# Attention scores as three 64-row products per head, two heads alternating on the halves of the array

## What is computed

```python
scale = d ** -0.5                      # d = 64
for blk in range(S // Q):              # blocks of 128 queries
    q0, q1 = blk * Q, (blk + 1) * Q
    logits = (jnp.einsum('bhtd,bhsd->bhts', q[:, :, q0:q1], k[:, :, :q1]) * scale
              + F[:, :, q0:q1, None] - F[:, :, None, :q1])
    probs = jax.nn.softmax(jnp.where(mask, logits, -jnp.inf), axis=-1)
    outs.append(jnp.einsum('bhts,bhsd->bhtd', probs, v[:, :, :q1]))
```

## Time and profile before

| | us |
|---|---|
| median of three runs | 3614.58 |
| lowest, highest | 3612.81, 3622.89 |
| span of the profiled execution | 3614.6 |
| TensorE busy in it | 3300.8 (91%) |
| VectorE, ScalarE, GpSimd busy | 1918.7, 1224.6, 881.6 |

### The profile page before, as it was taken

One profiled execution on the slowest core, in us unless ns is written; L12 is line 12 of the kernel. 1 busy time (PEld: TensorE's weight loads), 2 busy tenths in 40 slices (PEclk: granted clock), 3 DMA queues, 4 the chain that ended last, 5 costly groups with the idle time before them and its releaser, 6 DMA issues.

```text
span 3614.6 us, 53582 instructions
## 1 busy us (share of the span) xinstructions
PE 3300.8 (91%) x19064; PEld 2868.2 (79%) x19064; DVE 1918.7 (53%) x3829; ACT 1224.6 (34%) x2043; POOL 881.6 (24%) x324
## 2 busy tenths in 40 slices
PE   8999999888888888999799989999799999999997
PEld 6878888777777777877588878887688888888875
DVE  4676566566666666014655545544564444444444
ACT  3343344333333333012344434430243333344302
POOL 2454344422222222334211010013111111111120
PEclk9899999999999999999799999999699999999997
DMA  2011011222222224411200010042021111010321
GB/s 99 35 46 46 35 41 41 102 86 75 76 81 81 81 79 176 156 65 47 93 33 33 27 39 28 27 172 78 14 79 45 45 39 39 29 39 33 115 93 58
DMA packets 63267, 235.80 MB, mean 65 GB/s; under 512 B 7216, under 2 KB 8240, under 8 KB 62144
## 3 DMA queue, kind: packets, MB, share of 16 engines
q10 hardware_dynamic: 32352, 118.58, 8.7%
q1 hardware_dynamic: 30816, 115.91, 8.7%
HBM read 184.06 MB, written 50.40 MB: 65 GB/s over the span
## 4 chain that ended last, share of the span: by engine, by line
PE 62%; DVE 17%; issue 11%; DVEq 5%; ACT 4%; DMA 1%; ACTq 1%; SPq 0%
PE ps L163 33%; PE ps L725 10%; PE ps L702 6%; DVE fox_l L978 4%; PE ps L120 3%; PE ps L686 2%; PE ps L359 2%; PE ps L687 2%; DVEq L524 2%; DVE fx_k2b L992 1%; DVE lev L503 1%; DVE nf_tri L1002 1%; PE ps L709 1%; DVE lev L514 1%; PE ps L372 1%
## 5 line engine op out<-in xcount | busy, mean ns | idle before, releaser
L184 POOL TENSOR_TENSOR w_hi<-raw,small 128x1024 fp32r<-128x1024 f32 x160 | 459.8, 2874 | 2632.1 <-PE ps L163 2526.0
L186 POOL TENSOR_TENSOR w_lo<-raw,w_hi 128x1024 fp32r<-128x1024 f32 x160 | 422.1, 2638 | 22.8
L163 PE MATMUL ps<-u_hi,w_hi 128*128 128x512 f32 x1040 | 415.0, 399 | 12.4 <-DVE u_lo L243 7.8
L163 PE MATMUL ps<-u_lo,w_hi 128*128 128x512 f32 x1040 | 410.5, 395 | 0.0
L163 PE MATMUL ps<-u_hi,w_lo 128*128 128x512 f32 x1040 | 410.5, 395 | 0.0
L163 PE MATMUL ps<-nb_u_hi,w_hi 128*128 128x512 f32 (+1 forms) x640 | 241.0, 377 | 10.2 <-DVE nb_u_lo L1389 9.9
L163 PEld LDWEIGHTS ps<-u_hi,w_hi 128*128 128x128 f32 x1040 | 197.4, 190 | 61.7 <-issue 10.6
L163 PE MATMUL ps<-nb_u_hi,w_lo 128*128 128x512 f32 (+1 forms) x640 | 237.9, 372 | 0.0
L163 PE MATMUL ps<-nb_u_lo,w_hi 128*128 128x512 f32 (+1 forms) x640 | 237.6, 371 | 0.0
L163 PEld LDWEIGHTS ps<-u_hi,w_lo 128*128 128x128 f32 x1040 | 197.5, 190 | 44.3
L163 PEld LDWEIGHTS ps<-u_lo,w_hi 128*128 128x128 f32 x1040 | 197.7, 190 | 41.9
(11 more groups left out here) (326 smaller groups left out, 7355.5 us busy)
## 6 DMA issues: line engine op xcount, KB each, us to landing
raw<-in_w_stream SPq DMA_DIRECT2D x160, 512.0 KB, 3.5
ada_w<-in_w_ada ACTq DMA_DIRECT2D x48, 512.0 KB, 6.1
nf_b<-nf_rows ACTq DMA_DIRECT2D x16, 512.0 KB, 5.7
nb_bias<-in_rel_bias ACTq DMA_DIRECT2D x16, 448.0 KB, 3.5
y_parts<-wa_y_hi ACTq DMA_DIRECT2D x8, 640.0 KB, 3.0
y_parts<-wa_y_lo ACTq DMA_DIRECT2D x8, 640.0 KB, 4.1
la_out_yh<-y_parts SPq DMA_DIRECT2D x8, 640.0 KB, 10.0
la_out_yl<-y_parts SPq DMA_DIRECT2D x8, 640.0 KB, 11.2
```

Of the source, the lines that this page charges most:

```text
L163: mm = pe.matmul(out, w(slot, tiles[i]), u[:, first + i, cols], start=start and i == 0 and p == 0, stop=stop and i == len(tiles) - 1 and p ...
L184: pool.tensor_tensor(w_hi[:, s, :], raw[:, s, :], zero, ALU.add)
L186: pool.tensor_tensor(w_lo[:, s, :], raw[:, s, :], w_hi[:, s, :].bitcast(F32), ALU.subtract).then_inc(w_ready, 1)
```

## The change

The query parts become `q_hi` and `q_lo`, the key parts `k_hi` and `k_lo`, each with the pair's first head in rows 0 to 63 and the second in rows 64 to 127, as the projection leaves them. One operation of 128 rows makes each of them, where two or four of 64 rows stood. In wa the queries change so; its keys stay as they were (both halves hold the shared head). Scores are three products of 64 rows per head, hi x hi, lo x hi, hi x lo; the fourth partial sum is no longer made. The two heads alternate, product by product, on rows 0 to 63 and 64 to 127 of the array, each into its own PSUM banks. So a pair's scores are one group on TensorE, and `plan` puts both S steps of the next pair ahead of the transposes of an odd head step: S0 S1 T.. S2 S3 T.. T.. S4 S5. The group waits until all earlier shifts are done. In wa both heads' scores now wait for `a_g`, in nb for `b_vc`, for which only the second head's did.

```diff
-                self.steps = [("S", u) for u in range(min(ahead, self.NA))]
+                self.steps = [("S", u) for u in range(2)]
...
                 for u in range(self.NA):
-                    if u + ahead < self.NA:
-                        self.steps.append(("S", u + ahead))
+                    if u % 2 and u + 2 < self.NA:
+                        self.steps += [("S", u + 1), ("S", u + 2)]
...
-                    if step[0] == "S":
+                    if step[0] == "S" and step[1] % 2 == 0:
                         u = step[1]
                         blk = self.blocks[u // 2]
-                        pe.wait_ge(self.shifted, it * self.NA + max(u - 1, 0))
+                        pe.wait_ge(self.shifted, it * self.NA + u)
...
-                        q = self.q2[u % 2][:, blk["b"] * P:(blk["b"] + 1) * P]
-                        for pc, kc, n in blk["runs"]:
-                            o = ps[:, (u % 2) * 2 * CH + pc:(u % 2) * 2 * CH + pc + n]
-                            pe.matmul(o, q, k2a[u % 2][:, kc:kc + n], start=True, stop=False)
-                            mm = pe.matmul(o, q, k2b[u % 2][:, kc:kc + n], start=False, stop=True)
-                        mm.then_inc(self.scored, 1)
+                        qc = slice(blk["b"] * P, (blk["b"] + 1) * P)
+                        for i, (pc, kc, n) in enumerate(blk["runs"]):
+                            products = ((self.q_hi, k_hi), (self.q_lo, k_hi), (self.q_hi, k_lo))
+                            for p, (q, k) in enumerate(products):
+                                for hd in range(2):
+                                    r = rows_of(hd)
+                                    mm = pe.matmul(ps[:, hd * 2 * CH + pc:hd * 2 * CH + pc + n], q[r, qc],
+                                                   k[r, kc:kc + n], start=p == 0, stop=p == 2)
+                                    if p == 2 and i == len(blk["runs"]) - 1:
+                                        mm.then_inc(self.scored, 1)
...
-                for hd in range(2):
-                    for half in range(2):
-                        ins = dve.tensor_tensor(fx_k2b[hd][rows_of(half), :], bank(2, 2)[rows_of(hd)],
-                                                fx_k2a[hd][0:HD, :].bitcast(F32), ALU.subtract)
-                ins.then_inc(f_lo, 1)
+                dve.tensor_tensor(fx_k_lo[:], bank(2, 2), fx_k_hi[:].bitcast(F32), ALU.subtract).then_inc(f_lo, 1)
...
-                    wa.pe(pe, it, [wa_k2a[g // 2]] * 2, [wa_k2b[g // 2]] * 2, [(wa_v, rows_of(g // 2))] * 2,
-                          {("S", 0): [(a_lo, j * 5 + (g + 2))],
-                           ("S", 1): [(a_g, it + 1)]})
+                    wa.pe(pe, it, wa_k2a[g // 2], wa_k2b[g // 2], [(wa_v, rows_of(g // 2))] * 2,
+                          {("S", 0): [(a_lo, j * 5 + (g + 2)), (a_g, it + 1)]})
...
-                      {("S", 1): [(b_vc, it + 1)],
+                      {("S", 0): [(b_vc, it + 1)],
```

More of the change, by code:

```diff
@@ L920, in fox_pe @@
                 mm.then_inc(f_vt, 1)
-                fox.pe(pe, it, fx_k2a, fx_k2b, [(fx_v, rows_of(hd)) for hd in range(2)],
+                fox.pe(pe, it, fx_k_hi, fx_k_lo, [(fx_v, rows_of(hd)) for hd in range(2)],
                        {("S", 0): [(f_lo, it * 2 + 2)],
@@ L943, in fox_act @@
                 act.wait_ge(w_used, it * 4 + (U_FOX + 1))
[L944 to L946 removed]
+                nc.scalar.activation(fox.q_hi[:], bank(0, 2), ACT.Copy, scale=HD ** -0.5).then_inc(f_hi, 1)
                 act.wait_ge(fox.chunk, it * 4 + 2)
                 act.wait_ge(w_used, it * 4 + (U_FOX + 2))
[L949 to L952 removed]
+                nc.scalar.copy(fx_k_hi[:], bank(2, 2)).then_inc(f_hi, 1)
                 load_ada(1)
@@ L1492, in wa_act @@
                     act.wait_ge(a_turned, j * 5 + (g + 2))
-                    for hd in range(2):
-                        ins = nc.scalar.copy(wa.q2[hd][rows_of(hd), :], wa.y[rows_of(hd), :])
-                    ins.then_inc(a_hi, 1)
+                    nc.scalar.copy(wa.q_hi[:], wa.y[:]).then_inc(a_hi, 1)
                     act.wait_ge(wa.chunk, j * 20 + 2 * (4 + 2 * g))
@@ L1568, in build_program @@
         ph7 = ctx.enter_context(ExitStack())
[L1570 to L1571 removed]
+        nb_k_hi = sb("nb_k_hi", [P, TC], F32R, ph7)
+        nb_k_lo = sb("nb_k_lo", [P, TC], F32R, ph7)
         nb_v = sb("nb_v", [P, 10, P], at=ph7)
@@ L1603, in nb_pe @@
                 mm.then_inc(b_vt, 1)
-                nb.pe(pe, it, nb_k2a, nb_k2b, [(nb_v, rows_of(hd)) for hd in range(2)],
-                      {("S", 1): [(b_vc, it + 1)],
+                nb.pe(pe, it, nb_k_hi, nb_k_lo, [(nb_v, rows_of(hd)) for hd in range(2)],
+                      {("S", 0): [(b_vc, it + 1)],
                        ("V", 0): [(b_g, it + 1)]})
```

51 lines of the change are left out of this document (13 added, 38 removed).

## The result

The kernel after takes 4008.6 us (median of 4, 3995.6 to 4025.9) where the kernel before takes 3613.7 us (3603.1 to 3622.9). The ratio is 1.109, with an interval of 1.105 to 1.113: slower by 395 us. The forecast was 3855 us, in a range up to 3960. It had the direction and missed the size by 154 us. The profiled execution has a span of 4001.5 us, 387 more than before.

The account below looks back on a forecast made before the run. TensorE, busy 91% of the span, was taken as the bound. The terms -61+11+54+208-4+30 = +238 us on 3614.6 us gave 3853, stated as 3855 us (chance 0.48), with a range of 3765 to 3960 us.

Parts of the forecast that it names:

- The products, -61: Score products on TensorE: the two halves overlap fully, 182 us in place of 243, so -61 us.
- the second half's load, +11: Weight load of the second half at the head of each score group, half of 0.108 us x 208 pairs: +11 us.
- Between full and half array, +54: TensorE going over to 64 rows and back, 0.30 us x 208 pairs, 8 less in nb: +54 us.
- The order, +208: TensorE waits longer at transposes as ScalarE does both heads' exp before copying: +208 us, bounds +150 and +250.
- Fewer copies in fox, -4: VectorE's dropped subtractions at a fox iteration's head: 0.5 of 4.9 us gained, eight times, -4 us.
- The sum without the clock: The terms -61+11+54+208-4 for the attentions; fox, wa and nb iterations some 6, 10 and 9 us longer.
- The clock, +30: Lower TensorE clock after waits at the head of nearly every wa and nb iteration: 16x1.9 = +30 us, bounds 0 and +80.
- Loads in turn: Rival: every weight load of the score products takes its turn, +90 us on the sum, 3945 us; chance 0.24.
- no overlap: Rival: score products on the two halves do not overlap at all, +171 us on the sum, 4025 us; chance 0.10.
- Smaller waits: Rival: TensorE's waits come to half of the 208 us, with no clock loss, 3720 us; chance 0.12.
- Not slower: Rival: copies arrive in time, crossings and waits together under 0.29 us per pair, down to 3550 us; chance 0.06.
- The signs: Expected profile: nb 320-column pair scores 1.2 to 1.4 us, copy waits 50 to 70 us per stage, clock 0.5 at heads.

Follow-up runs that it names:

- e7: Kernel before with one 64-row product of 64 columns added ahead of each head's two whole-array score products; 3696.4 us.
- e5: Kernel after with whole-array products that nobody reads added where TensorE stands, ahead of the waits; 3827.6 us.
- e1: Kernel before with only the step order changed to that of after, old operands, products and copies kept; 3756.3 us.
- e6: Kernel before with each head's first score product done twice, so three whole-array products per head; 3695.8 us.
- e2: Kernel after with the old order restored and each head's three 64-row products done alone, without the other head's beside them; 4469.3 us.
- e14: Kernel before with the additions of both e6 and e7; 3794.1 us.
- e3: Kernel after with TensorE's paired products where they were, but VectorE and ScalarE taking the two heads' scores one transposing group apart; 3748.7 us.
- e4: Kernel after with whole-array products added behind the wait for the copies and ahead of the wait for the exp; 4013.1 us.
- e9: As e5, but each added product reads 64 rows instead of 128; 3862.3 us.
- e11: Kernel before with 26 products of 64 rows (rows 0 to 63) added at the head of each fox iteration, where TensorE stands; 3606.8 us.
- e15: Kernel after with every pair's six 64-row score products done twice, the first results overwritten; 4163.1 us.

## Why the prediction was right in direction and short in size

Point by point, with what the runs put against each term of its sum.

- **The products, -61, and the second half's load, +11.** Right. Places of 0.12 us for a pair of 256-wide products, 0.15 for 320; the first place of a group is 0.19, 0.07 more, 15 us over 208 pairs. The Trainium skill, TensorEngine Tiling (Array Packing), Key Properties (tiles run loads and products independently) is borne out by these rows, and TensorE: Matmul & The Clock Gate, Part 3, too, for two tiles.
- **Between full and half array, +54.** Right: 208 x 0.24 = 50 by e7. The 8 us taken off for the groups behind a 64-row chunk are doubtful: such a group takes 1.56 us instead of 1.35.
- **The order, +208.** Right. In after itself the standing grew by 168 us, presumably because a TensorE at half speed arrives later and so stands less. At full clock it is e5's standing and fill, 136 + 199 us (27, 25, 7, 24, 10 and 38 products of 0.23 or 0.17 us, eight times), less before's 134: 201 us. By stage these are 61, 72 and 68 us (forecast 54, 78 and 75). An upper bound, if a fill outlasts its wait. The order alone, on the old products, costs 144 us (e1).
- **Fewer copies in fox, -4.** Right. In after VectorE's one subtraction (1.21 us, 4.93 in the earlier trace rows) is followed by a stand for the ada weights, and from the first scores to the first shift are 6.20 us where 6.81 were: 0.6 of the possible 4.9.

```profile
1254.57 1.21 DVE L988 TENSOR_TENSOR fx_k_lo<-ps,fx_k_hi 128x1024 fp32r<-128x1024 f32 x1
1260.58 0.06 DVE L976 MEMSET ada_acc<- 128x1 f32 x1 [4.80 <-DMA ada_w<-in_w_ada]
```

- **The sum without the clock** was +208, and e5 has +216. By iteration it was 6, 10 and 9 us, and e5's iterations are 8.1, 11.6 and 7.6 us longer than before's.
- **The clock, +30, bounds 0 to 80.** This is the term that failed: 181 us (after less e5). The forecast took from the earlier trace rows what a low clock after a wait costs at the head of an iteration (1.6 us there, taken as 1.9), and counted heads. It didn't ask what the clock does in the body of an attention once TensorE stands 1 to 2.5 us at every pair and a part of what it does between is on half the array. Inside the attentions the time at the lower level went from 86 to 625 us. Nothing in the trace of before had that mix, so the bound of 80 had no ground: the nearest rows priced one wait and were multiplied by a count of places.
- **Rivals.** Loads in turn and no overlap: not so. The 0.108 us per load that priced the first is a little over the 0.10 that the forecast's own rows give. Their times, 3945 and 4025, lie on either side of the measured one by chance, and a reader who had only the time would have picked the wrong cause. Smaller waits: no. Not slower: no; the point from which it decides (crossings and waits under 0.29 us per pair) is far off: 0.24 for the crossing and 201/208 = 0.97 for the waits. Its chance stands as 0.06 among the rivals and as 0.05 in the line below them.
- **The signs.** The 320-wide group at 1.35 us (1.2 to 1.4 forecast): right where the clock was full and no 64-row chunk went before. At the lower level it is 2.37 us, over the 2 us that were named as a sign of being wrong; that sign holds at full clock only. The waits for ScalarE's copies, 50 to 70 us in each stage: 47, 22 and 32 us in fox, wa and nb, so too high, and in wa hardly over the 20 that would have spoken against it. The exps have 68, 22 and 20 us more, of which 60 are the wait at the head of a fox iteration: it moved there from the scores as said and grew by 0.7 us. The low clock at the heads: there, and not only there. Iterations 6, 10 and 9 us longer: 18.8, 16.6 and 14.3, the difference being the clock's.

What lowered the clock, as far as it is shown: not standing alone (e1), not changes of shape alone (e7), not the third product (e6); half-array products head by head alone do (e2 against e14); in after, where the halves overlap, they and the standing do it together, since taking either away restores most of it (e1, e5, and e3 in part). Whole-array work added for the most part outside the waits raised the clock too (e4). The Trainium skill, TensorE: Matmul & The Clock Gate, A second HAM failure mode: psum-queue depth-cycling, describes a clock that swings where TensorE idles briefly between groups of products. After agrees, e1 does not, with 0.945 at 255 us of such idling.

What stays open is the weight of a half-array product. e9 and e11 give it nearly that of the whole array in a gap, e2 gives it much less in a steady row, e15 is between.

## What to carry to other kernels

Two products side by side on the halves of the array save their columns, but a visit to the half array costs 0.24 us here (e7), and the pairing forces both heads' follow-up work into one place; count what TensorE then waits for before counting the columns. When an edit adds both idle time and partial-array work to a stage that ran at full clock, give the clock a term as large as the waits themselves (181 us beside 201 here) until a run says otherwise. If the products must be paired, let the other engines take the two results apart in time (e3 took back 260 of 395 us by that alone), and to split a slowdown into its own cost and the clock's, fill the waits with products that nobody reads.

## What the hardware showed that was not expected

- 215 us of whole-array products added to after, some 130 of them outside its waits, cost 5 us (e4), while the clock rose from 0.886 to 0.935.
- A TensorE that is busy for 98% of a stage was granted a clock of 0.66 when its score products used 64 rows one at a time (e2), and 1.00 with at least as many columns on 128 rows (e14).
- The executions of e2 differed by 5% (4361 to 4589 us) where every other kernel stayed within 1%.
- A group's first score product starts 0.15 us ahead of a value product that stands before it in the program, both of 64 rows (TensorE in after):

```profile
3580.36 0.38 PE L690 MATMUL ps<-nb_k_hi,nb_q_hi 64*128 64x256 f32 x1
3580.51 0.27 PE L730 MATMUL ps<-nb_v,nb_pt 64*128 64x64 f32 x1
```
